# Score masks added in PSUM by VectorE instead of by mask matmuls on TensorE

## The reference

```
# first layers: differential attention, 8 heads of 64, in blocks of 128 queries
s = einsum('bqgd,bkgd->bgqk', q_i, k)
allowed = key_chunk[None, :] <= query_chunk[:, None]      # chunks of 64 positions
s = where(allowed, s, -1e30); p = softmax(s); p = p[:, 0] - lam * p[:, 1]
# second layers: attention with 8 query heads on 2 key heads, two causal branches
# (selected blocks and a window), each a masked softmax of q.k
s = where(causal, q.k * scale, -1e30); p = softmax(s)
```

## Time and profile before

| | before |
|---|---|
| time, median of 3 runs (lowest to highest) | 2010.58 us (2009.91 to 2010.92) |
| time of the profiled execution | 2009.22 us |
| its span, first to last instruction | 2007.4 us |
| mean granted TensorE clock | 0.998 |
| TensorE busy | 1980.2 us, 99% |
| VectorE busy | 1263.8 us, 63% |
| ScalarE busy | 904.8 us, 45% |

### The profile page before, as it was taken

One profiled execution on the slowest core, in us unless ns is written; L12 is line 12 of the kernel. 1 busy time (PEld: TensorE's weight loads), 2 busy tenths in 40 slices (PEclk: granted clock), 3 DMA queues, 4 the chain that ended last, 5 costly groups with the idle time before them and its releaser, 6 DMA issues.

```text
span 2007.4 us, 31808 instructions
## 1 busy us (share of the span) xinstructions
PE 1980.2 (99%) x13856; PEld 1802.3 (90%) x13856; DVE 1263.8 (63%) x1790; ACT 904.8 (45%) x1188; POOL 72.8 (4%) x74
## 2 busy tenths in 40 slices
PE   8999999999999999999999999999999999999998
PEld 7888999999787999999899988799999998879997
DVE  6566666555656665655665567765566556776555
ACT  4445544444445444444344435444435444544442
POOL 0000001000100000100100010010010001001000
PEclk9999999999999999999999999999999999999999
DMA  7544556666543456686576655468657665546663
GB/s 288 168 146 142 181 197 195 206 206 190 175 163 132 166 175 199 189 251 189 168 217 190 187 153 158 106 191 244 189 170 225 186 189 150 149 107 193 189 189 105
DMA packets 421412, 361.84 MB, mean 180 GB/s; under 512 B 29392, under 2 KB 361496, under 8 KB 421272
## 3 DMA queue, kind: packets, MB, share of 16 engines
q1 hardware_dynamic: 421272, 359.80, 58.6%
HBM read 358.72 MB, written 1.05 MB: 179 GB/s over the span
## 4 chain that ended last, share of the span: by engine, by line
PE 89%; DVE 6%; ACT 2%; POOL 1%; DMA 1%; issue 1%; SPq 0%; DVEq 0%; ACTq 0%
PE ps L217 21%; PE ps L218 21%; PE ps L219 21%; PE ps L224 7%; PE ps L226 7%; PE ps L225 7%; PE ps L1488 2%; DVE hl L1997 2%; ACT hl L1776 1%; PE ps L1596 1%; DMA raw<-in_w_in 1%; POOL hl L1952 1%; PE ps L1630 1%; DVE xs L2057 0%; DVE small L2103 0%
## 5 line engine op out<-in xcount | busy, mean ns | idle before, releaser
L1997 DVE TENSOR_TENSOR hl<-raw,hl 128x1024 fp32r<-128x1024 f32 (+1 forms) x537 | 733.7, 1398 | 397.2 <-ACT hl L1776 395.9
L217 PE MATMUL ps<-xt,hl 128*128 128x256 f32 (+1 forms) x2672 | 755.2, 283 | 5.3 <-DVE hl L1997 5.3
L218 PE MATMUL ps<-xt,hl 128*128 128x256 f32 (+1 forms) x2672 | 746.9, 280 | 0.0
L219 PE MATMUL ps<-xt,hl 128*128 128x256 f32 (+1 forms) x2672 | 746.5, 279 | 0.0
L1776 ACT ACTIVATE hl<-raw 128x2048 fp32r<-128x2048 f32 (+1 forms) x323 | 612.3, 1900 | 224.1 <-PE ps L226 159.9
L217 PEld LDWEIGHTS ps<-xt,hl 128*128 128x128 f32 (+1 forms) x2672 | 501.7, 188 | 11.2 <-DVE hl L1997 5.7
L218 PEld LDWEIGHTS ps<-xt,hl 128*128 128x128 f32 (+1 forms) x2672 | 501.8, 188 | 3.1
L219 PEld LDWEIGHTS ps<-xt,hl 128*128 128x128 f32 (+1 forms) x2672 | 501.5, 188 | 0.2
L224 PE MATMUL ps<-hl,o 128*128 128x512 f32 x656 | 261.3, 398 | 0.0
L226 PE MATMUL ps<-hl,o 128*128 128x512 f32 x656 | 258.9, 395 | 0.0
L225 PE MATMUL ps<-hl,o 128*128 128x512 f32 x656 | 258.8, 394 | 0.0
(11 more groups left out here) (197 smaller groups left out, 1552.9 us busy)
## 6 DMA issues: line engine op xcount, KB each, us to landing
raw<-in_w_in SPq DMA_DIRECT2D x83, 1024.0 KB, 5.0
raw<-in_w_ffn_in SPq DMA_DIRECT2D x88, 512.0 KB, 5.1
raw<-in_ffn_gate SPq DMA_DIRECT2D x88, 512.0 KB, 3.9
raw<-in_ffn_up SPq DMA_DIRECT2D x88, 512.0 KB, 5.2
raw<-in_ffn_down SPq DMA_DIRECT2D x44, 1024.0 KB, 5.0
raw<-in_w_ffn_out SPq DMA_DIRECT2D x22, 1024.0 KB, 5.1
raw<-in_w_out SPq DMA_DIRECT2D x24, 512.0 KB, 4.8
raw<-in_w_branch_a SPq DMA_DIRECT2D x8, 1024.0 KB, 5.0
```

Source lines behind the costliest of these rows:

```text
L217: e.matmul(out, l[0], r[0], start=start, stop=False)
L218: e.matmul(out, l[0], r[1], start=False, stop=False)
L219: return e.matmul(out, l[1], r[0], start=False, stop=stop)
L1997: e.tensor_tensor(lo[:, c], m["raw"][:, k % NRAW, 0:n][:, c], hi[:, c].bitcast(F), ALU.subtract).then_inc(s.low.up(("low", k), *([("low", ...
```

## The change

The 48 mask matmuls go, and with them the step `masks`. The last score matmul of a bank now signals that the bank is full. VectorE adds the mask, in float32 from the table of constants and broadcast over the two heads, onto the last 128 keys of both heads in the PSUM bank itself: one instruction over 128x256 elements that reads PSUM and the table and writes PSUM. It then waits for that instruction and takes the maximum as before. The two masks in the table are turned, since the matmul had transposed them. Nothing else is moved: the list of steps is the same apart from `masks`, and so are the banks that it hands out.

```
     put("decay", dec * 128 ** -0.5)
-    put("chunk", np.where((p[:, None] >= 64) & (p[None, :] < 64), NEG, 0.0))
-    put("causal", np.where(p[:, None] > p[None, :], NEG, 0.0))
+    put("chunk", np.where((p[:, None] < 64) & (p[None, :] >= 64), NEG, 0.0))
+    put("causal", np.where(p[:, None] < p[None, :], NEG, 0.0))
...
-        if l == 0:
-            add("masks")
...
     # TensorE
-                ins = e.matmul(b.ap[:, n * K:(n + 1) * K], qs[n][hh], ks[n][hh], start=n == 0, stop=mask is None and n == 1)
-                if mask is None and n == 1:
+                ins = e.matmul(b.ap[:, n * K:(n + 1) * K], qs[n][hh], ks[n][hh], start=n == 0, stop=n == 1)
+                if n:
                     ins.then_inc(done.up(b.full), 1)
-        for hh, b in enumerate(bs):
-            if mask is not None:
-                ins = e.matmul(b.ap[:, 0:2 * K].rearrange("p (n k) -> p n k", n=2)[:, :, 128 * i:K], mask, bc(m["maskb"][:, 0, :], 1, 2),
-                               start=False, stop=True)
-                ins.then_inc(done.up(b.full), 1)
...
     # VectorE
-    def soft(b, n, K, nm, er, rs):
+    def soft(b, n, K, mask, nm, er, rs):
+        masked = b.ap[:, 0:n * K].rearrange("p (n k) -> p n k", n=n)[:, :, K - 128:K]
+        e.wait_ge(*T["const"])
         e.wait_ge(*T[b.full])
+        e.tensor_tensor(masked, masked, bc(mask, 1, n), ALU.add).then_inc(done.up(), 1)
+        e.wait_ge(*done.now)
         e.tensor_reduce(nm, b.ap[:, 0:n * K].rearrange("p (n k) -> p n k", n=n), AX, ALU.max, negate=True).then_inc(done.up(("max", b.n)), 1)
```

More of the change, by code:

```diff
@@ L453, in script @@
     add = P.add
-    identb, chunkb, causalb = m["maskb"][:, 0, :], m["maskb"][:, 1, :], m["maskb"][:, 2, :]
+    chunk, causal = C("chunk"), C("causal")
     def xt_i(v, i, c):
@@ L724, in score_pair @@
         add("score_pair", bs, [[q[64 * hh:64 * hh + 64, j, i * 128:(i + 1) * 128] for hh in range(2)] for j in js],
-            [[k(hh, j)[:, 0:K] for hh in range(2)] for j in js], mask, i, q_events)
+            [[k(hh, j)[:, 0:K] for hh in range(2)] for j in js], q_events)
         for hh in range(2):
@@ L729, in score_pair @@
             else:
-                add("soft", bs[hh], 2, K, P.small(2), ers[hh], rs[hh])
+                add("soft", bs[hh], 2, K, mask, P.small(2), ers[hh], rs[hh])
         PB.give(*bs)
@@ L988, in task @@
                 rs, rc = P.small(4), P.small(4)
-                e0, e1 = score_pair(q0, K, js, i, None, chunkb, [[rs[:, 2 * hh + n:2 * hh + n + 1] for n in range(2)] for hh in range(2)],
-                                    [("q da", l, 1), ("k da", l, 1), "masks"])
+                e0, e1 = score_pair(q0, K, js, i, None, chunk, [[rs[:, 2 * hh + n:2 * hh + n + 1] for n in range(2)] for hh in range(2)],
+                                    [("q da", l, 1), ("k da", l, 1)])
                 mixed = ("da mixed", l, P.new())
@@ L1283, in task @@
                     yield from at.until("q")
-                ers = score_pair(Q, K, js, i, None, causalb, [[rs[:, 2 * hh + n:2 * hh + n + 1] for n in range(2)] for hh in range(2)],
-                                 [("q nsa", l, jp), ("k nsa", l), "masks"])
+                ers = score_pair(Q, K, js, i, None, causal, [[rs[:, 2 * hh + n:2 * hh + n + 1] for n in range(2)] for hh in range(2)],
+                                 [("q nsa", l, jp), ("k nsa", l)])
                 yield 1.1 + 0.5 * i
@@ L1586, in ffn_down, with score_pair @@
         ins.then_inc(done.up(b.full, *events), 1)
-    def score_pair(bs, qs, ks, mask, i, events):
-        K = 128 * (i + 1)
+    def score_pair(bs, qs, ks, events):
         for x in events:
@@ L1595, in score_pair @@
                     e.wait_ge(*T[b.before])
-                ins = e.matmul(b.ap[:, n * K:(n + 1) * K], qs[n][hh], ks[n][hh], start=n == 0, stop=mask is None and n == 1)
-                if mask is None and n == 1:
+                K = ks[n][hh].shape[1]
+                ins = e.matmul(b.ap[:, n * K:(n + 1) * K], qs[n][hh], ks[n][hh], start=n == 0, stop=n == 1)
+                if n:
                     ins.then_inc(done.up(b.full), 1)
-        for hh, b in enumerate(bs):
-            if mask is not None:
-                ins = e.matmul(b.ap[:, 0:2 * K].rearrange("p (n k) -> p n k", n=2)[:, :, 128 * i:K], mask, bc(m["maskb"][:, 0, :], 1, 2),
-                               start=False, stop=True)
-                ins.then_inc(done.up(b.full), 1)
     def weigh(tb, blocks, er, er_event, et, flip):
@@ L1984, in start @@
         e.memset(m["zb"][:, :, 0:2], 0.0).then_inc(done.up("zpad"), 1)
[L1986 to L1991, removed]
     def low(k, n, h, parts):
@@ L2363, in cmp_turn @@
                         ALU.mult).then_inc(done.up(et.full, tb.free), 1)
-    run(steps, dict(start=start, masks=masks, low=low, turn_split=turn_split, o_split=turn_split, scale=scale, rotate=rotate, silu_gate=silu_gate, ln_stats=ln_stats,
+    run(steps, dict(start=start, low=low, turn_split=turn_split, o_split=turn_split, scale=scale, rotate=rotate, silu_gate=silu_gate, ln_stats=ln_stats,
                     ln_norm=ln_norm, ln_split=ln_split, ln_last=ln_last, ffn_gate=ffn_gate, ffn_turn=ffn_turn,
```

## The result

The changed kernel takes 2019.51 us (median of 6 runs, 2018.7 to 2020.15), the kernel before, beside it on the same chip, 2010.24 (6 runs, 2009.7 to 2012.54). The ratio is 1.0045, with an interval of 1.0034 to 1.0056: slower by 9.3 us, where 4.2 were forecast and 2018.0 was the top of the range. The profiled execution took 2018.93 us with a span of 2017.1.

What follows compares the result with a forecast made beforehand. TensorE, busy 99% of the span, was taken as the bound on average, its chain leaving it once per second layer. Second layers +5.1 and first layers -1.0 made +4.2 us on 2010.58: 2014.8, range 2009.5 to 2018.0.

Steps and rivals of the forecast that it cites:

- The saving: TensorE, all score pairs: dropping the mask matmuls saves 0.12 us a pair, 2.9 us at most.
- all is kept: First layers, 8 pairs: VectorE's lag goes in its waits, so the whole saving stays, -1.0 us.
- The add's price: VectorE, each bank: one add costs 0.45 us up to the reduction, 0.90 a pair.
- the dearer write: Rival, VectorE's add: writing PSUM makes it 0.52 us or more, time 2016.7 upward; chance 0.08.
- VectorE absorbs it: Rival, second layers: idle VectorE takes up its lag, only the saving stays, 2007.7 us (2010.6 with last chain late); chance 0.17.
- Pairs 1 to 4: Second layer: late exponentials hold the bank for the transposes behind pair 4, leaving TensorE 1.55 us late.
- Last pair: End of a second layer's attention: the chain through VectorE and ScalarE comes 1.02 us late and TensorE stands longer.
- The sum for a second layer: Each second layer's attention: 1.55 + 1.02 = 2.6 us longer, twice 5.1.
- The clock rival: Rival, behind the last pair's stall: TensorE's clock falls, 1.5 us in each layer, time 2016.3 or 2017.8; chance 0.22.
- the same shift gives 2014.8: Whole kernel: the profiled execution's distance of 1.4 us under the median is carried over unchanged, from 2013.4 to 2014.8.
- ledger: Second layers: running account of how late each engine is against the earlier profile; forecast 2013.0 to 2016.5, chance 0.50.

Runs made afterwards that it cites:

- e12: Changed kernel with mask matmuls back in the second layers, plus 8 unread matmuls before one projection at 759 us: 2011.83 us, ratio 1.0013.
- e3: Changed kernel with mask matmuls put back in the first layers, adds in the second layers only: 2017.84 us, ratio 1.0032.
- e13: Changed kernel, but second layers' adds write the whole row to SBUF, freeing the bank after the add: 2023.02 us, ratio 1.0064.
- e1: Changed kernel unchanged, run and profiled once more: 2019.78 us.
- e6: Changed kernel with 20 unread matmuls put at the projection of the values, which doesn't wait: 2022.88 us.
- e10: Changed kernel with 20 unread matmuls at the wait for weights in each second layer: 2015.67 us, ratio 1.0029.
- e14: Kernel before, unchanged, profiled once more: 2012.82 us.
- e9: Kernel before with 20 unread matmuls at the wait for weights in each second layer: 2009.01 us, ratio 0.9994.
- e11: Changed kernel with mask matmuls back in the second layers and 20 unread matmuls at both waits for weights: 2007.31 us, ratio 0.9989.
- e15: Changed kernel with mask matmuls back for second layers' pairs 1 to 4 and 8, 20 unread matmuls at both waits for weights: 2008.54 us, ratio 0.9990.
- e2: Changed kernel with mask matmuls put back in the second layers, adds in the first layers only: 2012.32 us, ratio 1.0005.
- e4: Changed kernel without adds or mask matmuls, masks left out of the computation: 2009.67 us, ratio 0.9992.

## Why the prediction was wrong

The direction and the mechanism were right: VectorE's adds cost more than TensorE's matmuls gave, in the second layers alone, at the transposes behind pair 4 and at the last pair. The size was not: +9.3 us for +4.2. Between the two profiled spans it is +9.8, 5.6 more than forecast: 3.7 of that outside the attentions, 1.2 in them, and 0.7 up to 1200.

- **The saving** of 0.12 a pair measured 0.13 as a step of the shift at each of the first layers' eight pairs. Right as a price. That "all is kept" was not: in the ten profiles without these matmuls (e12, delayed, aside) the shift moved by -0.6 to -0.8 us from 170 to 1200, not by -1.0, against -0.1 to +0.1 in those with them. Behind the first wait for weights nothing of it is to be seen: from 170 to the matmul behind this wait the shift moved by +0.1 us on average in those ten (-0.5 to +0.9), and by +0.2 in the six with the matmuls.
- **The add's price** of 0.45 measured 0.46, by the adds' own rows. Right; the dearer write falls. The Trainium skill ("Perfetto Trace Analysis", Optimizing Scalar/DVE Operations) sets VectorE's access to PSUM some 60 ns over that to SBUF; these rows, 425 and 422 ns, don't show it.
- **VectorE absorbs it** fell with e3: 6.0 us, though VectorE is idle for more than a third of the span. The rule that the prediction takes for this rival from the Trainium skill ("Perfetto Trace Analysis") stands there in the section Identifying the Most-Contended Engine.
- **Pairs 1 to 4**: 1.92 late behind pair 3 was forecast, 1.93 came. The 1.55 for TensorE came as 1.73 in layer 3 (shift 1.15 when the attention begins, 2.88 behind the transposes), but in two parts: first 0.82 us at a projection in front, which VectorE's late copy ended, and then 1.17 at the transposes. The first wait was not foreseen. It adds nothing to the sum, since the second is the shorter for it. That the second is for the bank is shown by e13, which shows too that without it TensorE waits for the same exponentials a little later.
- **Last pair**: 1.02 forecast, 1.1 in layer 3 and 1.4 in layer 4 measured; in e3 1.1 in both. The 0.3 more are not the clock's: in the four profiles with adds in all layers (after, e1, e6, e10) VectorE stands 0.58 to 0.59 us in layer 4 in front of the reciprocals ahead of the last pair's adds, and 0.23 in e3. Why is open.
- **The sum for a second layer**, 2.6, is therefore a term sized too small: 2.7 to 3.7 in ten attentions with all eight adds (after, e1, e3, e6, e10), 2.8 to 3.2 in the five of them without half clock behind the last pair. That is 0.2 to 0.6 us, twice.
- **The clock rival** named the wrong place. I gave it 1.5 us behind the last pair's stall. It falls there in five of those ten attentions, but costs 0.4 to 0.5 (layer 4: the shift rises from 9.41 to 10.84 over the slow matmuls and is back at 9.76 behind the next transposes, in front of which TensorE otherwise stands 0.68 us for VectorE and now doesn't wait). The dear places are the waits for weights, 1.41 us for 3.41 of half clock at 1208.
- **The step that failed** is the one that carried all else over unchanged: "the same shift gives 2014.8". The earlier trace rows showed two waits, one with and one without half clock behind it, and I took this as the state of the kernel, where it is that of one execution. Between the two profiles that step missed 3.7 us: 10.24 us of half clock behind the two waits instead of 3.41, and a second wait 1.05 us longer. It is not shown that the change brings this. Against e14, which has the changed kernel's 10.24 us of half clock behind the waits, the changed kernel's profile is 6.1 us longer: -0.7 up to the first attention, +2.82, +0.5 between, +3.52.

The Trainium skill ("TensorE: Matmul & The Clock Gate", HAM oscillation) describes a kernel whose TensorE idles at DMA waits and starts the next piece at the lower clock. The traces agree by e9 to e11 and e15; but the wait's length alone doesn't decide, since 3.5 us (e3) had none of it behind and 2.4 (e12) had.

**What stays open.** Between 6.1 to 6.7 us with the clock taken out or alike and the 9.3 measured lie about 3 us. They may go with half clock, by the mean clocks, where 0.001 is an estimated 2 us of TensorE's time (0.001 of 2010): all six runs of the changed kernel have a mean clock of 0.996, while of 23 runs of before beside e2 to e4 three had 0.998, 17 had 0.997 and three 0.996. Adds in the first layers alone go with more of it too (eight of e2's 11 runs at 0.996), yet e4, without mask matmuls there either, has 0.997 or 0.998 in all ten. Whether the change makes the stretch likelier is not settled. Behind the first wait, unfilled, it is there in all eight profiles without mask matmuls in the first layers, and in one of five with them. A delay of 0.94 us didn't take it away (e12), which doesn't show that no other delay would. Nor is it settled why that wait lasts from 2.8 to 4.1 us.

## What to carry to other kernels

Work taken from the busiest engine is worth its distance between starts (0.13 us a pair here), and is kept only if no later wait takes it back; work given to an engine with 36% idle time still costs where that idle time is a wait for a third engine that is itself late. Before a ledger is set against one profile, take a second profile of the same kernel: here two of the same program differ by 3.7 us in places that no change touched. A wait that the data make unavoidable can be filled with matmuls that nobody reads. That kept the clock whole behind both waits in all four profiles; in time it is not clear of no change (2.0 us by medians of 11 and 30 runs; ratio 0.9994, 0.9985 to 1.0003), though about as much as leaving the masks out gave (e4).

## What the runs showed of the hardware

- The half-clock stretches in mid-run last 3.41 us or twice that, whatever the wait in front (2.4 to 4.1 us).
- The same program has the stretch in one execution and not in another: behind 1209 before had none, e14 3.41 us; the changed kernel 3.41 and 6.83.
- In front of the first wait for weights, ScalarE waits for a weight transfer and starts 10.1 to 11.8 us after SyncE issued the rows for the normalization in front of it; its wait scatters from 6.6 to 8.3 us between executions. The attentions with mask matmuls are steady to 0.03.
- A VectorE add of 128x256 float32 takes 425 ns from PSUM to PSUM, a product of that shape from SBUF to SBUF 422.
